# A two-layer model step on one core: recurrence outputs grouped by kind, key products on ScalarE, routing inside the output projection

## The reference

```
# delta rule per head and direction, chunks of 64 tokens
v_new = u_c - w_c @ S
o_c   = q_c @ S + qk_c @ v_new            # a product with the state, one with the values
S     = S * exp(gl) + k_c.T @ v_new       # k_c = k_dec, the key product
...
h = h + concat(o_delta, o_pool) @ w_out   # output projection
xn = rmsnorm(h, norm_ffn)
probs = softmax(xn @ router_w)            # 256 x 16
gate, idx = top_k(probs.T, 32)            # each expert picks its tokens
y = (silu(xn[idx] @ w_gate) * (xn[idx] @ w_up)) @ w_down * gate
out = rmsnorm(h + scatter_add(y, idx), norm_final)
```

## Time and profile before

| | us |
|---|---|
| three runs | 2174.59, 2176.62, 2167.54 |
| median | 2174.59 |
| the profiled execution's own time | 2171.24 |
| its span, first to last instruction | 2169.4 |
| TensorE busy | 1646.8 |
| VectorE busy | 740.1 |
| ScalarE busy | 443.5 |
| GpSimd busy | 321.4 |
| moved by DMA | 738.56 MB |

### The profile page before, as it was taken

The page is one execution under the profiler, slowest core; times in us unless marked ns, Lnnn a source line. Parts: engine busy times, 40 slices in busy tenths (PEclk is TensorE's granted clock), DMA queues, the critical chain, the costliest instruction groups (busy, mean ns, idle before and its releaser), DMA issues. The chain is left out here.

```text
span 2169.4 us, 23762 instructions
## 1 busy us (share of the span) xinstructions
PE 1646.8 (76%) x9138; PEld 791.6 (36%) x9138; DVE 740.1 (34%) x1685; ACT 443.5 (20%) x956; POOL 321.4 (15%) x315
## 2 busy tenths in 40 slices
PE   6998879879777877779898666666666666667665
PEld 6987755445333333339686410111111011111110
DVE  3256266777777766654652200000000000000001
ACT  4256233322223222234320200000000000000001
POOL 0042023424433333310130000000000000000000
PEclk9999989989998999999899787877876777877777
DMA  6451469999999999976003699999999999999997
GB/s 243 132 176 59 146 275 383 419 420 421 419 421 421 421 420 421 421 290 242 2 3 140 285 420 419 420 420 421 420 421 421 420 420 421 420 421 421 420 420 314
DMA packets 111666, 738.56 MB, mean 340 GB/s; under 512 B 14048, under 2 KB 15712, under 8 KB 27616
## 3 DMA queue, kind: packets, MB, share of 16 engines
q1 hardware_dynamic: 74432, 468.91, 53.4%
q0 software_dynamic: 36864, 268.45, 29.9%
q10 hardware_dynamic: 288, 0.08, 0.0%
HBM read 736.35 MB, written 1.05 MB: 340 GB/s over the span
## 5 line engine op out<-in xcount | busy, mean ns | idle before, releaser
L2416 PE MATMUL ps<-arena,xe 128*32 128x512 f32 x2048 | 376.4, 826 | 202.3 <-DMA arena<-in_experts_in 200.7
L1088 PE MATMUL ps<-arena 128*128 128x512 f32 x820 | 401.3, 639 | 115.8 <-ACT arena L1267 115.0
L2487 DVE TENSOR_TENSOR low<-low,ps 128x512 f32<-128x512 f32 x16 | 11.0, 688 | 889.8 <-PE ps L2416 889.8
L1473 DVE CUSTOM_DVE_ANT_0 arena<-arena,ps 128x1024 f32<-128x1024 f32 x205 | 247.8, 1219 | 127.2 <-DMA arena<-in_peer,arena 122.6
L1088 PEld LDWEIGHTS ps<-arena 128*128 128x128 f32 x820 | 161.8, 203 | 336.1 <-issue 190.4
L988 POOL DMA_INDIRECT arena<-in_peer,arena x205 | 196.5, 959 | 430.5 <-PE ps L1088 330.5
L2416 PEld LDWEIGHTS ps<-arena,xe 128*32 128x32 f32 x2048 | 48.5, 123 | 519.4 <-DMA arena<-in_experts_in 496.6
L2440 PE MATMUL ps<-arena,hT 128*32 128x512 f32 x1024 | 165.2, 747 | 78.8 <-DMA arena<-in_experts_down 67.1
L2516 POOL TENSOR_TENSOR low<-h,hT 128x512 f32<-128x512 f32 x2 | 2.5, 1273 | 945.6 <-DVE h L2500 945.6
L1267 ACT ACTIVATE arena<-ident,arena 128x128 f32<-128x128 f32 x256 | 83.7, 391 | 150.4 <-DVE arena L1483 145.9
L2440 PEld LDWEIGHTS ps<-arena,hT 128*32 128x32 f32 x1024 | 25.8, 122 | 200.3 <-DMA arena<-in_experts_down 161.2
(11 more groups left out here) (434 smaller groups left out, 1958.4 us busy)
## 6 DMA issues: line engine op xcount, KB each, us to landing
arena<-in_experts_in SPq DMA_DIRECT2D x256, 1024.0 KB, 26.9
arena<-in_experts_down SPq DMA_DIRECT2D x128, 1024.0 KB, 27.1
ring<-in_stream SPq DMA_DIRECT2D x44, 512.0 KB, 4.3
arena<-in_stream SPq DMA_DIRECT2D x36, 512.0 KB, 4.1
arena<-in_stream SPq DMA_DIRECT2D x14, 1024.0 KB, 7.0
arena<-in_peer,arena POOLq DMA_INDIRECT x205, 26.8
h<-in_x SPq DMA_DIRECT2D x1, 1024.0 KB, 5.2
arena<-in_sel SPq DMA_DIRECT2D x1, 1024.0 KB, 5.7
```

The costliest lines, as they stand in the source:

```text
L1088: last = nc.tensor.matmul(ps[:, 4 + 2 * t + half, :], diag[:, n % DIAGS, :], slot(n)[:, D + half * BANK:D + (half + 1) * BANK], start=firs ...
L1473: nc.vector.tensor_tensor_reduce(slot(n)[:, 0:D], slot(n)[:, 0:D], xrow(j // (QUADS // NT)), 1.0, 0.0, ALU.mult, ALU.add, act_in[:, u % 2, ...
L2416: last = nc.tensor.matmul(ps[32 * j:32 * (j + 1), 4 + r // KB, :], xe[:, k, :], w[:, j * BANK:(j + 1) * BANK], start=(k == 0), stop=(k == ...
```

## The change

Four things change; the arithmetic stays, except that the router multiplies `h` with the norm's gain and applies the norm's root to the logits instead of to the tokens.

1. In the inversion `kdec` and `kb_` are made on ScalarE, in 32 pieces of 128x128, two per step from step 4 to step 19. `vb` stays on VectorE in steps 12, 15, 18 and 21. GpSimd only masks.
2. `outputs` makes the four products with the state together and the four with the values together; which come first is set so that neighbours are of one kind.
3. Projection, routing and experts are one block. `project`, `turn` (transposes of `h`) and `route` (router's products) are interleaved on TensorE. Squares and half of the copies into `hT` are ScalarE's, the sums and the other half VectorE's. The first expert's pieces come between the gather groups, behind the third of them, each with its own copy of `xe`.
4. The expert ring's first lap has two more places: `spare_piece` takes piece 14 and `hT` piece 15, so pieces 16 and 17 find places 14 and 15 of `arena` free. Behind the first lap the ring has 16 places again, shifted by two.

```diff
 class ExpertRing:
+    def place(self, i, pair):
+        if isinstance(pair, int) and pair == 0 and i < RING3:
+            return i
+        return (i - len(self.extra)) % RING3
+    def before(self, i):
+        place = self.place(i, 0)
+        return i - RING3 if i >= 2 * RING3 or place >= RING3 - len(self.extra) else place
...
 # inversion, GpSimd
-                if 12 <= n < 16:
-                    g = n - 12
-                    nc.gpsimd.tensor_tensor(grp(kdec, g), tok2[:, 0, g // 2, :, :],
...
 # inversion, ScalarE, behind the copy pb(n)
+                for u in range(2 * (n - 4), min(2 * (n - 4) + 2, 2 * NU)):
+                    dst, by = ((kdec, scal[:, 2, :]), (kb_, scal[:, 3, :]))[u // NU]
+                    v = u % NU
+                    nc.scalar.activation(dst[:, v, :], tok2[:, 0, v // 8, v % 4, :], ACT.Copy, scale=by[:, v:v + 1])
 # inversion, VectorE
-                if 8 <= n < 16:
-                    g = n % 4
...
+                if n >= 12 and n % 3 == 0:
+                    g = n // 3 - 4
...
 # recurrence
+            def outputs(st, d, state_first):
...
+                if st == 0:
+                    last = from_values(True)
+                elif state_first:
+                    from_state(True)
+                    last = from_values(False)
+                else:
+                    from_values(True)
+                    last = from_state(False)
...
-                    outputs(st - 1, 1)
+                    outputs(st - 1, 1, True)
-                outputs(st, 0)
+                outputs(st, 0, st == 3)
-            outputs(3, 1)
+            outputs(3, 1, False)
...
 # SyncE, the one block
+            for i in range(4):
+                sync.wait_ge(ring2.used, G2_EXP - RING2 + i + 1)
+                first_lap(i)
+            for i in range(RING2, RING3 - 1):
+                first_lap(i)
+            for i in range(4, RING2):
+                sync.wait_ge(ring2.used, G2_EXP - RING2 + i + 1)
+                first_lap(i)
+            for i in range(RING3, RING3 + 2):
+                first_lap(i)
+            sync.wait_ge(logits, 1)
+            first_lap(RING3 - 1)
...
+            for q in range(RING3 + 2, PAIR):
+                sync.wait_ge(ring.used, ring.before(q) + 1)
                 load(q, 0)
 # TensorE
+            project(0)
+            project(1)
+            turn(0)
+            project(2)
+            turn(1)
+            pe.wait_ge(c3, 16 * len(loads))
+            route(0)
+            project(3)
+            turn(2)
+            route(1)
+            turn(3)
+            route(2)
+            route(3)
...
                 for r in range(2 * KB):
                     q = odd * PER + r
+                    if opening and r + 2 < KB:
+                        gather(r + 2)
+                    if opening and r < KB:
+                        pe.wait_ge(xe_first, r + 1)
...
 # ScalarE
+            square(0)
+            square(1)
+            keep_left(0)
+            square(2)
+            keep_left(1)
+            keep_left(2)
+            square(3)
+            keep_left(3)
```

More of the change, by code:

```diff
@@ L2225, in _, with experts @@
             nc.scalar.activation(orn[:, :, :], orn[:, :, :], ACT.Sqrt).then_inc(on_rt, 1)
[L2227 to L2250, removed]
-                nc.vector.tensor_tensor(x, x, ps[:, c, :].rearrange("p (t c) -> p t c", t=NT), ALU.add).then_inc(res2, 1)
     stack.close()
-    experts(T)
-def experts(T):
+    experts(T, oT)
+def experts(T, oT):
     nc, A, ps, sem = T.nc, T.A, T.ps, T.sem
-    h, hT, ident, ring = T.h, T.hT, T.ident, T.expert_ring
+    h, hT, ident, ring, ring2 = T.h, T.hT, T.ident, T.expert_ring, T.ring2
     expert_stack = ExitStack()
@@ L2290, in small @@
-    def small(pe, done):
-        pe.wait_ge(c3, 16 * len(loads))
-        for t in range(NT):
-            for k in range(KB):
-                last = nc.tensor.matmul(ps[:, 4, t * NEXP:(t + 1) * NEXP], hT[:, k, t * P:(t + 1) * P], router_w[:, k, :],
-                                        start=(k == 0), stop=(k == KB - 1))
-        last.then_inc(done, 1)
-    front(T, "ec", 3, T.ring2, G2_EXP, [], small, refill, xs=xs)
+    res2, sq_sum, turned, hT_act, hT_dve, logits, mean_in, root_in, r_in = (sem(f"rt_{n}") for n in (
+        "res", "squares", "turned", "h_act", "h_dve", "logits", "mean", "root", "r"))
@@ L2387, in _, with first_lap @@
         def _(sync):
+            for dst, name in loads:
+                sync.dma_start(dst, A[name]).then_inc(c3, 16)
+            def first_lap(i):
+                src = A["experts_in"][0, i // KB, i % KB] if i < 2 * KB else A["experts_down"][0, i - 2 * KB]
+                sync.dma_start(ring.piece(i, 0), src).then_inc(ring.sem_of(i, 0), 16)
+            for i in range(4):
[10 more added lines that the diff above has]
+            first_lap(RING3 - 1)
             def load(q, pair):
@@ L2398, in _ @@
                 for q in range(PAIR):
+                    sync.wait_ge(ring.used, pair * PAIR + (q - RING3 + 1))
                     load(q, pair)
@@ L2406, in _, with project @@
         def _(pe):
+            def project(c):
+                ring2.arrived(pe, G2_OUT + c)
+                w = ring2.piece(G2_OUT + c).rearrange("p (k c) -> p k c", k=KB)
+                for t in range(NT):
+                    for k in range(KB):
+                        last = nc.tensor.matmul(ps[:, c, t * S:(t + 1) * S], oT[:, k, t * P:(t + 1) * P], w[:, k, :],
+                                                start=(k == 0), stop=(k == KB - 1))
+                last.then_inc(ring2.used, 1)
@@ new lines, in route @@
+            def route(c):
+                pe.wait_ge(res2, 2)
+                pe.wait_ge(hT_act, c + 1)
+                pe.wait_ge(hT_dve, c + 1)
+                for t in range(NT):
+                    for k in (2 * c, 2 * c + 1):
+                        last = nc.tensor.matmul(ps[:, t, 0:NEXP], hT[:, k, t * P:(t + 1) * P], router_w[:, k, :],
+                                                start=(k == 0), stop=(k == KB - 1), skip_group_check=True)
+                if c == 3:
+                    last.then_inc(logits, 1)
```

235 lines of the change are left out of this document (144 added, 91 removed).

## The result

| | before | after |
|---|---|---|
| median of the runs, us | 2173.61 | 2147.72 |
| lowest and highest | 2167.54, 2176.62 | 2144.58, 2152.12 |
| the profiled execution | 2171.24 | 2147.29 |
| its span | 2169.4 | 2145.5 |

The ratio is 0.9886, with a 95% interval from 0.9858 to 0.9914 (four runs of each). The forecast was 2143.0 with a range from 2136 to 2154. Between the two profiled executions the time fell by 23.95 us; the forecast for that difference was 28.1.

The account below looks back on a forecast made before the run. The prediction took the expert weight stream, waiting for its first free ring place, to bound the kernel. Gains of 2.1 + 6.6 + 7.0 + 1.2 + 6.2 + 5.0 = 28.1 us from 2171.24 gave 2143, range 2136 to 2154.

Parts of the forecast that it names:

- The frame: Expert weight stream: end is time of first free place, plus 2.498 us per piece not yet in, plus 20.1 us.
- the last piece at 2123: End of the expert weight stream: a sign to look for, the last piece arriving at 2123 us.
- Part 1: Inversion, ahead of the output projection: key products on ScalarE are hidden and remove stretched steps, 2.1 us less.
- Part 2: Recurrence, ahead of the output projection: outputs grouped by kind avoid 39 gaps of 0.17 us, 6.6 us less.
- -6.6: Recurrence: microseconds saved by grouping outputs, taken in full as lying on the path; the other bound was 0.
- the gaps stay: Rival, recurrence: each weight load waits for the matmul before it despite grouping; only 21.5 us left, 2150; 8%.
- Part 3: Output projection's start (S) to first free place: routing inside the projection and earlier first use, 14.4 us nearer, S + 56.2.
- Logits: Projection and routing: logits there 38.0 us behind the projection's start instead of 45.0, a gain of 7.0 us.
- Logits to gather: From logits to gather: earlier table load and reordered copies and transposes, 1.2 us less, between 0 and 1.6.
- First use: Gather to first free place: first expert piece behind three gather groups, 5.4 us instead of 11.6, 6.2 less.
- Part 4: Expert ring: two more places, so 18 pieces in before first use instead of 16, 5.0 us less.
- The sum: Whole kernel: all terms together 28.1 us less than the profiled 2171.24 us, giving 2143.1.

Follow-up runs that it names:

- before_b: The kernel before, unedited, in a further profile (one execution, third job): 2173.07 us.
- no_route: The kernel before with only the grouped outputs, ScalarE's key products and the new places of `vb`; routing and ring as before: 2165.75 us, ratio 0.9964.
- no_places: The kernel after without the two more ring places, 16 from the start: 2148.30 us, ratio 0.9885.
- experiment 3: The kernel after with key products back on GpSimd and VectorE: 2146.79 us, ratio 0.9887; repeated 2145.70 us.
- again: The kernel after, unedited, run once more: 2142.31 us, ratio 0.986.
- experiment 6: The kernel after with all eight gather groups ahead of the first expert piece: 2146.54 us, ratio 0.9871.
- experiment 5: The run `no_places`: the kernel after with a ring of 16 places from the start, 2148.30 us, ratio 0.9885.
- again_b: The kernel after, unedited, in a further profile (one execution, third job): 2145.27 us.

## Why the prediction was right, and what was wrong in it

**The frame.** The end is the time of the first free place plus a length fixed by the pieces not yet in. In all 14 profiled executions the span behind the first free place is 936.9 to 938.0 us with 16 pieces in before it (`before`, `before_b`, `no_route`, `no_places`) and 932.5 to 934.0 with 18, though the first free place itself moves between 1201.92 and 1234.26. The mechanism is shown; every other term is a question of when that place comes free.

One row was misread. The product at 2151.11 is not the last piece's: the products that combine the experts stand ahead of the last two, which follow in this row of the timeline of before:

```profile
2155.87 1.92 PE L2440 MATMUL ps<-arena,hT 128*32 128x512 f32 x16
...
2156.33 0.13 PEld L2440 LDWEIGHTS ps<-arena,hT 128*32 128x32 f32 x4 [0.30 <-DMA arena<-in_experts_down]
```

The weight load of the last piece ends its wait for the transfer at 2156.33. The pace is therefore (2156.33 - 1231.78) / 368 = 2.512 us a piece and the tail 14.9, not 2.498 and 20.1. The two errors cancel: two pieces are 5.02 us, and the sum is untouched. The forecast of the last piece at 2123 meant the other row and can't be compared; by the right one it came at 2132.79.

**Part 1: right.** Forecast 2.1, measured 2.1 us as a mean (experiment 3), 2.0 between the first two profiles. Behind the first seven or eight steps of the inversion nearly all are 1.40 us apart (in the profile after one takes 1.84).

**Part 2: the mechanism right, its setting wrong.** Grouping is worth 7.0 us at the full clock. The step that failed is "-6.6" as a sum against the profiled execution of before, in which the clock happened to stay at 1.00: the text never asked at which clock the stage would run. In the profiled execution after it fell for 14 us, and the stage took 31.0 instead of 24.7: 6.3 us given back. Where the fall lasted 3 us (`again`, `no_places`) 1.6 us went. The row on what TensorE does just ahead of it is the same in before, where the clock held, and in after, where it fell. Timeline of before, then of after:

```profile
1126.44 1.68 PE L2137 MATMUL ps<-tok,low 64*128 64x128 f32 x16 [1.34 <-DVE tok L2175]
```

```profile
1123.65 1.68 PE L2177 MATMUL ps<-tok,low 64*128 64x128 f32 x16 [1.34 <-DVE tok L2215]
```

Of 12 profiled executions without filler six had the fall, `before_b` among them. Grouping can't set it off, since it begins ahead of the first products that are grouped. Whether grouping makes it last longer, or ScalarE's products make it likelier, is open: it came in five of eight executions with grouping (3 or 14 us) and in one of four without (7 us), and likewise in five of eight with ScalarE's products and in one of four without. These are too few to tell. What sets it off was not found. The rival "the gaps stay" would have read 31.7 us and 0.17 us gaps; without the repeats the 31.0 of the first profile would have been taken for it.

The Trainium skill (TensorE: Matmul & The Clock Gate, Part 3, The mechanism) has a weight load overlap running products only if it goes to another row group. The prediction concluded that mixed kinds should overlap better. That does not follow: weights of 128 rows share rows with any others in either order, so by this rule alone the order makes no difference, which is the result that the rival priced. Here the mixed order took 31.74 us and the grouped one 24.72, so the rule does not cover these products; the gaps go with a change of the weights' shape.

**Part 3: the sum right, two terms wrong against each other.** S to the first free place shrank by 15.0 us, forecast 14.4.
- Logits: S + 35.9, forecast 38.0. I had the routing products at 1.34 us per group of four, from rows of a stretch partly at the lower clock. In the projection the clock is 1.00 from its second part on, and a group takes 0.96, a group of transposes 0.60 instead of 0.84. Against that the first quarter took 10.0 us, not 9.1. Timeline of after:

```profile
1181.57 0.96 PE L2386 MATMUL ps<-router_w,hT 128*128 128x16 f32 x8
```

- Logits to gather: forecast 1.2 us less, measured none. The exponential did start right behind its input. But a tiny conversion that took 0.17 us before now takes 1.44. Timeline of before:

```profile
1209.89 4.50 POOL L2351 TENSOR_TENSOR xs_parts<-low,xs_parts 128x2048 fp32r<-128x2048 f32 x1 [96.09 <-ACT xs_parts L2343]
...
1215.20 0.17 DVE L2326 CAST place_f<-place 16x32 f32<-16x32 uint32 x1
```

Timeline of after:

```profile
1193.76 0.23 ACT L2509 ACTIVATE probs<-probs 128x32 f32<-128x32 f32 x1 [0.18 <-DVE probs L2565]
...
1198.09 4.50 POOL L2624 TENSOR_TENSOR xs_parts<-low,xs_parts 128x2048 fp32r<-128x2048 f32 x1 [87.10 <-ACT xs_parts L2513]
...
1201.18 1.44 DVE L2581 CAST place_f<-place 16x32 f32<-16x32 uint32 x1
1202.65 0.68 DVE L2582 TENSOR_TENSOR diag<-place_f,ident 16x512 f32<-16x512 f32 x1
```

  GpSimd's subtraction starts later against VectorE's chain than before, behind the two scaled copies now ahead of it on ScalarE, and is still running when the conversion starts: it ends at 1202.59, the conversion at 1202.62. I had asked only whether the subtraction is done before the gather, not what runs beside it. In `again` the conversion starts at 1196.07 and takes 1.65, and the subtraction ends at 1197.69, the conversion at 1197.72. So in all 11 profiled executions with the new routing: 1.44 to 1.65 us, ending within 0.05 of GpSimd's end; in the three with the old one the subtraction was over and the conversion took 0.17. The Trainium skill (SBUF — State Buffer, Who interferes with whom) says that VectorE and GpSimd share a pair of ports, that conversions are among the operations that can take it, and that whichever comes second waits for the whole of the first; these rows fit. No run moved the subtraction by itself, so the cause is read from rows and not tested.
- First use: 5.7 us, forecast 5.4; the three gather groups took 4.7 us instead of 4.3. Experiment 6 shows that the order is what brought the gain.

**Part 4: right, a little too high.** Forecast 5.0, shown by experiment 5 as 4.4 us in the profiles' last stretch; over the 12 profiles without filler that stretch is 937.5 us on average with 16 pieces in and 933.3 with 18, 4.2 us. Where the last 0.6 to 0.8 us went is open. The stream did stand still for about 6 us, as forecast, so the 18 pieces were in.

**The sum** against the profiled executions: ahead of S 4.1 (forecast 8.7): 0.8 from an earlier start of the inversion, which is no part of the change, 2.0 in it, 0.7 in the recurrence and 0.6 from the transposes to S. Then S to the first free place 15.0 (14.4) and behind it 4.8 (5.0). Together 23.9 of 28.1. That no more than 4.2 us are missing is in part luck: the clock cost 6.3 us, which the sum did not hold, and 1.4 of the 4.1 us ahead of S (the earlier start and the 0.6) belong to none of its terms. Where the clock held, as in `again_b`, S came at 1154.20, although the inversion began at 1080.79, 3.6 us later than in after.

## What to carry to other kernels

Where a stream of transfers sets the end, find the first moment at which it waits for a place, and count the pieces in by then: everything else is hidden, and two small places more are worth nearly two pieces. In a stage that TensorE bounds with small fp32 products, put products whose weights have one shape behind each other. Before a stage of tens of microseconds is costed from one profile, look at the granted clock in more than one execution of it, and at what a moved operation will newly run beside, not only at whether it is done in time.

## What was not expected of the hardware

- The granted clock fell to 0.50 for 3, 7 or 14 us in the recurrence in six of 12 profiled executions without filler, of either kernel, always 0.3 to 2.5 us behind the start of the first key products. In the 10 us ahead of these TensorE had waited longer than 0.2 us only twice, for 0.8 and 1.3 us, in all 12 alike. It costs 1.6, about 3.2 and 6.3 us.
- Products that compute nothing made the next stage faster: 32 of them in two waits took 3.5 us off the stretch from S to the first free place.
- A conversion of 16x32 numbers on VectorE takes 0.17 us, and 1.44 to 1.65 us beside a GpSimd subtraction of 128x2048, until that ends; finds of maxima and replacements beside the same subtraction kept their 0.40 to 0.42 us.
